# Nine token blocks of two widths (504 and 368) instead of nine of 460, a weight ring of six places instead of nine, and convolution sums written over their own input

## The chip, the cores and the metric

The kernel runs on one core of one Trainium2 chip. The metric is the device time of one execution in microseconds (us), from the first to the last instruction and what lies around them; lower is better. Several executions are timed and the median counts; one more is recorded by the profiler.

## The reference

One layer of a streaming encoder and a final RMSNorm, in float32, for a prompt of 4096 frames and a running stream of 32 more ("sample"), 4128 tokens in all:

```python
D_MODEL = 1024; D_A = D_B = 512; D_IN = 4 * D_A + 3 * D_B        # 3584
hn = rms_norm(x, norm_g)
proj = jnp.einsum('btd,de->bte', hn, w_in)
h_a, b_a, c_a, z_a, a_b, g_b, z_b = jnp.split(proj, SPLITS, axis=-1)
conv_a, new_a = causal_dwconv(hist_a, c_a * h_a, conv_a_w)       # 3 taps
out_a = b_a * conv_a * jax.nn.silu(z_a)
v_b = a_b * jax.nn.sigmoid(g_b)
conv_b, new_b = causal_dwconv(hist_b, v_b, conv_b_w)             # 31 taps
s_b = jax.nn.silu(layer_norm(conv_b + conv_b_bias, ln_b_g, ln_b_b))
out_b = s_b * jax.nn.silu(z_b)
mixed = jnp.concatenate([out_a, out_b], axis=-1)
y = rms_norm(x + jnp.einsum('bte,ed->btd', mixed, w_out), final_norm_g)
```

The outputs are y for both streams and the last 2 and 30 input rows of the two convolutions.

## The kernel before, in words

**Products.** Each float32 product is made of three matmuls on rounded halves (high by high, high by low, low by high), in `split_product` (L1933, L1934, L1935), so every operand of TensorE (PE) has a high part, made by ScalarE (ACT), and a low part, made by VectorE (DVE) or GpSimd (POOL) as a difference. A matmul here is 128 stationary columns against one block of tokens: its moving operand is as wide as the block.

**Blocks, units and periods.** The 4128 tokens and 12 columns of padding make nine blocks of TB = 460. The input projection runs in five units of 14 periods (`ORDER`, `ORDER4`); a period makes one pair of 128-channel tiles of the projection (`ga` the gated input of the 31-tap convolution, `hc` that of the 3-tap one, `bz` and `zz` the gates).
- Unit 0 (periods 0 to 13) is blocks 0 and 1, computed plainly: four tiles of 24 matmuls a period, 1344 in all; the first two tiles are 448 wide, since the padding is left out. Beside it the weights of each period are loaded, split and added up into the seven forms that Strassen's scheme needs, and stored to DRAM (`weight_forms`).
- Units 1 to 3 (periods 14 to 55) are two blocks each by one level of Strassen's scheme: seven products (P1 to P7) of 12 matmuls instead of eight, 84 matmuls a period, 3528 in all. The weight form of each product comes back from DRAM into `w_ring`, a ring of nine places, in the order of the products; a load waits for the product that held its place.
- Unit 4 (periods 56 to 69, "late") is the last block, computed plainly: 48 matmuls a period, 672 in all, as 56 half tiles. Their weights are loaded raw (`load_late`), then split by ACT and POOL (`late_low`).
- The output stage multiplies `mixed` by `w_out` in row tiles of 128 tokens, 48 matmuls of 512 columns each, with the LayerNorm steps of a token block `L` of 512 in between. Its first row tiles need the LayerNorm of block 0 (`first_ln`), which DVE does in periods 63 to 69, and whose last step `b_low` (L1765) releases the second group of matmuls.

**DVE.** For each of the 20 jobs (a unit by a group of 128 channels) DVE makes 31 taps, each one instruction as wide as the unit (L1701 the first, L1704 the others), that add into PSUM; the last tap writes `conv_b_out`, which is stored to DRAM. DVE works strictly in program order: how many taps stand in each period is a number of `tap_quota` (10 in most periods of units 0 to 3, 12 in unit 4, 7 in period 55), and a job's taps can't begin before its input `v` is made. Beside the taps stand the low parts of the weights (L1534), the 3-tap convolution (L1647, L1650), the products of tiles (L1612 to L1668), and at the ends of the units the sums and low parts of the next unit's x (L1543 to L1562).

**SyncE (SP)** issues all DMAs in one order, and waits in it.

Of the kernel before, what the change touches and what calls it, by code (L numbers as in the profile page):

```python
# [10 lines left out]
P = 128  # L11
# [10 lines left out]
BLOCKS = 9  # L22
TB = 460
PAD = BLOCKS * TB - SEQ - SAMPLE
S0, P0 = PAD, PAD + SAMPLE
TOK = BLOCKS * TB
STAT_COLS = 4
STAT_ROWS = TB // STAT_COLS
# [114 lines left out]
ACC_W = [SAMPLE + HB + 2 * TB - P0, 2 * TB, 2 * TB, 2 * TB, TB]  # L143
CA_W = [SAMPLE + HA + 2 * TB - P0, 2 * TB, 2 * TB, 2 * TB, TB]
VW, UW = 968, 928
VP, UP = HB + SAMPLE + HB, HA + SAMPLE + HA
BLK0 = TB - P0


def tap_quota(n):  # L150
    u, g = divmod(n, G14)
    if n == 0:
        return 0
    if n == III - 1:
        return 7
    if g == G14 - 1 and u < 3:
        return 1
    if g == 0 and u < 4:
        return 3
    return 10 if u < 4 else 12  # L160
# [33 lines left out]
ACC_BANK, STAT_BANK = 6, 7  # L194
FIRST_BANK = [7, 6]
# [3 lines left out]
def build_program(nc, A):  # L199
    ctx = ExitStack()  # L200
    with ctx:
# [9 lines left out]
        def sem(name):  # L211
# [5 lines left out]
        rstd_d = nc.dram_tensor("rstd_spill", [1, BLOCKS * P * STAT_COLS], F32).ap()  # L217
# [30 lines left out]
        acc = sb("conv_b_out", [P, 944], F32, early)  # L248
        sets = sb("sets", [P, 2, 4, TB], F32, early)
        ca = sb("conv_a_acc", [P, 2 * TB], F32, early)  # L250
        u = sb("u", [P, UW], F32, early)
        row = sb("x_row", [P, D], F32, early)
        spread = sb("rstd_spread", [P, TB + 4], F32, early)
        xf, xf_f32 = sb_two("xf", [P, 7, 2 * HALF, TB], early)
        st = sb("x_raw", [P, 4, HALF, TB], F32, early)
        ring, ring_f32 = sb_two("w_ring", [P, 9, 2, HC], early)
        early.close()

        sb("late_gap_a", [P, 2 * VW + 944])
# [13 lines left out]
        MIX = [mix1, mix2]  # L273
        MIX_F32 = [mix1_f32, mix2_f32]
# [1924 lines left out]
```

## Time and profile before

| | |
|---|---|
| three timed runs | 1564.76, 1566.05, 1567.96 us; median 1566.05 |
| profiled execution | 1561.36 us, of which span 1559.6 us |
| PE busy | 99% of the span |
| granted clock, mean | 0.999 of full speed |
| unit 0 begins, ends | 23.8, 301.5 us |
| units 1 to 3 end | 1041.5 us |
| unit 4 and the first output matmuls end | 1190.4 us |

The profiled execution is 4.7 us below the median. The span is cut by the starts of PE's first matmuls of a unit. PE's records of one matmul overlap, so its own cost is read as the distance between the starts of two, or as a stretch of time divided by the matmuls in it.

### The profile page before, as it was taken

To read this page: it belongs to the slowest core of one execution; us is meant where nothing else is said; L and a number is where in the kernel's file an instruction comes from. 1 tells how busy PE (TensorE), PEld (TensorE's weight loads), DVE (VectorE), ACT (ScalarE), POOL (GpSimd) and SP (SyncE) were. 2 spreads that over 40 slices of the span, in tenths; PEclk is the share of its full clock that TensorE was granted. 3 is DMA by queue.
4 is the path that set the end of the run, shared out by engine and by line. 5 is a ranking of instruction groups with operands and counts; after the bars stand their busy time and mean duration, and the time that the engine had idled before them with its cause. 6 is when DMAs were issued, how large, how long until landed. Compare 5 with 4: busy or idle time off the path is not lost. (4 is left out here: it accounts for less than half of the span.)

```text
span 1559.6 us, 19243 instructions
## 1 busy us (share of the span) xinstructions
PE 1537.6 (99%) x7244; PEld 1358.4 (87%) x7244; DVE 1262.9 (81%) x1175; ACT 537.6 (34%) x780; POOL 578.4 (37%) x494
## 2 busy tenths in 40 slices
PE   6999999999999999999999999999999999999998
PEld 6999999988888888888888888888898888888886
DVE  7699799998878998869798888789896677787853
ACT  5443433332242333332253312234533323323221
POOL 2766969112313121132221141146964233332320
PEclk9999999999999999999999999999999999999999
DMA  4987978788987789897779877757645433445441
GB/s 164 337 320 279 339 266 317 261 276 287 292 276 241 232 250 301 288 289 247 233 231 298 255 239 246 215 174 221 203 121 192 162 126 138 168 162 188 142 142 69
DMA packets 109648, 358.03 MB, mean 230 GB/s; under 512 B 16676, under 2 KB 20644, under 8 KB 105976
## 3 DMA queue, kind: packets, MB, share of 16 engines
q1 hardware_dynamic: 109560, 356.86, 68.8%
q8 instruction: 55, 0.90, 0.2%
q14 instruction: 33, 0.27, 0.0%
HBM read 263.02 MB, written 93.79 MB: 229 GB/s over the span
## 5 line engine op out<-in xcount | busy, mean ns | idle before, releaser
L1704 DVE SCALAR_TENSOR_TENSOR ps<-v,conv_b_taps,ps 128x920 f32<-128x920 f32 (+2 forms) x580 | 630.9, 1088 | 17.8
L1933 PE MATMUL ps<-xf,w_ring 128*128 128x460 f32 (+1 forms) x1624 | 602.8, 371 | 1.0 <-issue 0.8
L1935 PE MATMUL ps<-xf,w_ring 128*128 128x460 f32 (+1 forms) x1624 | 602.6, 371 | 0.0
L1934 PE MATMUL ps<-xf,w_ring 128*128 128x460 f32 (+1 forms) x1624 | 600.8, 370 | 0.0
L1933 PEld LDWEIGHTS ps<-xf,w_ring 128*128 128x128 f32 x1624 | 305.4, 188 | 35.2 <-issue 2.1
L1934 PEld LDWEIGHTS ps<-xf,w_ring 128*128 128x128 f32 x1624 | 305.4, 188 | 34.0
L1935 PEld LDWEIGHTS ps<-xf,w_ring 128*128 128x128 f32 x1624 | 304.9, 188 | 34.2
L1268 ACT ACTIVATE sets<-ps 128x460 f32<-128x460 f32 x168 | 92.9, 553 | 488.7 <-PE ps L1935 488.5
L1074 POOL TENSOR_TENSOR sets<-sets 128x460 f32<-128x460 f32 x42 | 56.2, 1337 | 414.9 <-ACT sets L1268 414.9
L1933 PE MATMUL ps<-w_out_split,mixed 128*128 128x512 f32 x528 | 206.0, 390 | 0.0
L1934 PE MATMUL ps<-w_out_split,mixed 128*128 128x512 f32 x528 | 205.7, 390 | 0.0
L1935 PE MATMUL ps<-w_out_split,mixed 128*128 128x512 f32 x528 | 205.5, 389 | 0.0
L1933 PEld LDWEIGHTS ps<-w_out_split,mixed 128*128 128x128 f32 x528 | 99.1, 188 | 21.2 <-DVE mixed L1765 0.5
L1935 PEld LDWEIGHTS ps<-w_out_split,mixed 128*128 128x128 f32 x528 | 99.1, 188 | 20.8
L1934 PEld LDWEIGHTS ps<-w_out_split,mixed 128*128 128x128 f32 x528 | 99.1, 188 | 20.5
L1477 ACT ACTIVATE ps<-h_rows 128x1024 f32<-128x1024 f32 x32 | 33.0, 1030 | 200.0 <-DVE h_rows L1851 200.0
L945 POOL TENSOR_TENSOR row_mean_sq_eps<-row_mean_sq,rms_eps 128x1 f32<-128x1 f32 x32 | 8.4, 264 | 228.4 <-ACT ps L1477 228.3
L1014 POOL TENSOR_TENSOR w_ring<-w_ring_f,w_ring 128x512 fp32r<-128x512 f32 x56 | 74.8, 1355 | 43.6 <-ACT w_ring L1228 43.6
L1933 PE MATMUL ps<-xf 128*128 128x448 f32 (+1 forms) x224 | 82.7, 369 | 0.0
L1935 PE MATMUL ps<-xf 128*128 128x448 f32 (+1 forms) x224 | 82.6, 369 | 0.0
L1934 PE MATMUL ps<-xf 128*128 128x448 f32 (+1 forms) x224 | 82.2, 367 | 0.0
L971 POOL TENSOR_TENSOR x_raw<-x_raw,rstd_spread 128x460 f32<-128x460 f32 x56 | 66.5, 1220 | 40.2 <-DMA rstd_spread<-rstd_spill 40.2
(166 smaller groups left out, 1650.2 us busy)
## 6 DMA issues: line engine op xcount, KB each, us to landing
w_ring<-weight_forms SPq DMA_DIRECT2D x294, 512.0 KB, 5.3
x_rows_again<-in_x_prompt SPq DMA_DIRECT2D x32, 512.0 KB, 4.3
out_y_prompt<-h_rows SPq DMA_DIRECT2D x32, 512.0 KB, 3.0
weight_forms<-xf SPq DMA_DIRECT2D x7, 2048.0 KB, 13.3
weight_forms<-w_ring SPq DMA_DIRECT2D x7, 2048.0 KB, 14.7
w_ring_f<-in_w_in SPq DMA_DIRECT2D x56, 256.0 KB, 3.1
xf_f<-in_w_in SPq DMA_DIRECT2D x26, 512.0 KB, 9.0
x_row<-in_x_prompt SPq DMA_DIRECT2D x28, 460.0 KB
```

The source lines that it names most:

```text
L945: pool.tensor_tensor(mean_sq[0:rows, r:r + 1], ssq[0:rows, r:r + 1], add, ALU.add).then_inc(h_ms, 1)
L971: pool.tensor_tensor(part, part, spread[:, 0:TB], ALU.mult).then_inc(x_scaled, 1)
L1014: pool.tensor_tensor(ring[:, slot, 1, :], ring_f32[:, slot, 1, :], ring[:, slot, 0, :].bitcast(F32), ALU.subtract).then_inc(late_lo, 1)
L1074: pool.tensor_tensor(sets[:, s, QC, :], sets[:, s, QC, :], sets[:, s, QD, :], ALU.add).then_inc(c22_made, 1)
L1268: act.activation(sets[:, n % 2, quarter, :], ps[:, bank, 0:TB], ACT.Copy).then_inc(copied, 1)
L1477: act.activation(out_pair(2)[0:rows, :], hrow[0:rows, s, :], ACT.Square, scale=RMS_SCALE, accum_out=ssq[0:rows, s:s + 1]).then_inc(h_sumsq, 1)
L1704: dve.scalar_tensor_tensor(dst, window, wb[:, j, k:k + 1], part, ALU.mult, ALU.add).then_inc(taps_done, 1)
L1933: pe.matmul(out, ahi, bhi, start=(start and x == 0), stop=False, skip_group_check=goes_on)
L1934: pe.matmul(out, ahi, blo, start=False, stop=False, skip_group_check=goes_on)
L1935: mm = pe.matmul(out, alo, bhi, start=False, stop=(stop and x == len(terms) - 1), skip_group_check=goes_on)
```

## The change

- **Widths.** Blocks 0, 1 and 8 (units 0 and 4) are 368 tokens, blocks 2 to 7 (the Strassen units) 504. There is no padding. The number of matmuls is the same. The taps are 766, 1008 and 368 columns wide instead of 938, 920 and 460.
- **Taps.** `tap_quota` gives 9 instead of 10 in the middle periods of unit 0. The last tap writes into `v`, over its own input, and `conv_b_out` is gone; `v` then waits for that store, two jobs earlier.
- **Ring.** `w_ring` has six places. The weight forms of unit 0 that had lain in it lie in `xf` now, the raw weights in four halves of the ring.
- **Unit 4.** Of its 56 half tiles, 21 load their weights from the stored forms (`late_form`), already split; 35 are still split anew.
- **Places.** The buffers of the output stage are laid out anew, the halves of `mixed` apart.

```diff
-BLOCKS = 9
-TB = 460
-PAD = BLOCKS * TB - SEQ - SAMPLE
+BLOCKS, TB, PAD = 1, SEQ + SAMPLE, 0
+NARROW, WIDE = 368, 504
+WIDTH = [NARROW] * 2 + [WIDE] * 6 + [NARROW]
+UNIT_WIDTH = [NARROW, WIDE, WIDE, WIDE, NARROW]
-ACC_W = [SAMPLE + HB + 2 * TB - P0, 2 * TB, 2 * TB, 2 * TB, TB]
+ACC_W = [HB + 2 * NARROW, 2 * WIDE, 2 * WIDE, 2 * WIDE, NARROW]
 def tap_quota(n):
-    return 10 if u < 4 else 12
+    return 9 if u == 0 else 10 if u < 4 else 12
+SLOTS = 6
-        acc = sb("conv_b_out", [P, 944], F32, early)
-        ring, ring_f32 = sb_two("w_ring", [P, 9, 2, HC], early)
+        ring, ring_f32 = sb_two("w_ring", [P, SLOTS, 2, HC], early)
+        def late_form(r):
+            return r % 4 == 0 or (r % 4 == 3 and r >= 2 * G14)
         def wait_v_free(eng, job):
-                eng.wait_ge(taps_done, KB * (job - 1))
+                eng.wait_ge(conv_out, conv_sent(job - 2))
             def load_w(g):
-                    done = 1 if g == 2 else g
-                    sp.wait_ge(w_sum, 4 * done)
-                    sp.wait_ge(w_lo_w, 2 * done)
+                    sp.wait_ge(w_sum, 4 * (g - 1))
+                    sp.wait_ge(w_lo_w, 2 * (g - 1))
-                if q >= 9:
-                    sp.wait_ge(product_done, q - 8)
+                if q >= SLOTS:
+                    sp.wait_ge(product_done, q - SLOTS + 1)
             def load_late(r):
+                if late_form(r):
+                    load_ring(g, r % 4, late_slot(r))
+                    return
             def tap(job, k):
-                dst = acc[:, 0:w] if k == KB - 1 else part
+                dst = v[:, job % 2, 0:w] if k == KB - 1 else part
             def standing_part(n, t, rs):
-                    mm = split_product(ps[:, bank_of(n, t), cols], terms, r == 0, r == 3)
+                    mm = split_product(ps[:, bank_of(n, t), 0:NARROW], terms, r == 0, r == 3)
             def late_tile(n, t):
-                    pe.wait_ge(late_lo, r + 1)
+                    if late_form(r):
+                        pe.wait_ge(ring_in[late_slot(r)], late_weights_in(r))
+                    else:
+                        pe.wait_ge(late_lo, LATE_AT[r])
```

**DVE at the boundary of unit 3 and unit 4.** Rows of its order before, from the low parts of the last block's x to the first taps of unit 4 (`ps` is the sum in PSUM, a name with a width each):

```order
L1569 TENSOR_TENSOR xf<-x_raw,xf 128x1840 x2
L1704 SCALAR_TENSOR_TENSOR ps<-v,conv_b_taps,ps 128x920 x7
L1577 TENSOR_TENSOR sets<-ps,sets 128x460
L1580 TENSOR_TENSOR sets<-ps,sets 128x460
L1668 TENSOR_TENSOR conv_a_acc<-ps,conv_a_acc 128x460
L1687 TENSOR_TENSOR sets<-conv_a_acc,sets 128x920
L1704 SCALAR_TENSOR_TENSOR ps<-v,conv_b_taps,ps 128x920 x4
L1704 SCALAR_TENSOR_TENSOR conv_b_out<-v,conv_b_taps,ps 128x920
L1621 TENSOR_TENSOR v<-ps,sets 128x460
L1701 TENSOR_SCALAR ps<-v,conv_b_taps,conv_b_bias_sb 128x460
L1704 SCALAR_TENSOR_TENSOR ps<-v,conv_b_taps,ps 128x460 x11
```

The same place of the changed kernel:

```order
L1605 TENSOR_TENSOR xf<-x_raw,xf 128x1472 x2
L1741 SCALAR_TENSOR_TENSOR ps<-v,conv_b_taps,ps 128x1008 x7
L1613 TENSOR_TENSOR sets<-ps,sets 128x504
L1616 TENSOR_TENSOR sets<-ps,sets 128x504
L1704 TENSOR_TENSOR conv_a_acc<-ps,conv_a_acc 128x504
L1723 TENSOR_TENSOR sets<-conv_a_acc,sets 128x1008
L1741 SCALAR_TENSOR_TENSOR ps<-v,conv_b_taps,ps 128x1008 x9
L1741 SCALAR_TENSOR_TENSOR v<-v,conv_b_taps,ps 128x1008
L1657 TENSOR_TENSOR v<-ps,sets 128x368
L1738 TENSOR_SCALAR ps<-v,conv_b_taps,conv_b_bias_sb 128x368
L1741 SCALAR_TENSOR_TENSOR ps<-v,conv_b_taps,ps 128x368 x11
```

Ahead of unit 4's first `v` DVE has ten wide taps where it had five, since unit 0 has 108 taps instead of 113 and the later periods the same number as before; and each is wider.

**SP at the same place.** Its last loads of unit 3 and the first of unit 4 before:

```order
L692 DMA w_ring<-weight_forms 128x1024
L714 DMA w_ring_f<-in_w_in 128x512 x9
L767 DMA w_out_split_f<-in_w_out 128x1024
L714 DMA w_ring_f<-in_w_in 128x512 x3
L728 DMA outa_spill<-sets 128x920
```

And in the changed kernel:

```order
L736 DMA w_ring<-weight_forms 128x1024 x5
L759 DMA w_ring_f<-in_w_in 128x512 x3
L736 DMA w_ring<-weight_forms 128x1024
L759 DMA w_ring_f<-in_w_in 128x512
L810 DMA w_out_split_f<-in_w_out 128x1024
L759 DMA w_ring_f<-in_w_in 128x512 x2
L736 DMA w_ring<-weight_forms 128x1024
L771 DMA outa_spill<-sets 128x1008
```

Every fourth of unit 4's loads is a form of 512 KB instead of 256 KB raw, and the loads run six places ahead of PE instead of nine.

## Rows read from the trace of the kernel before

**Rows 1.** The page, parts 1 and 2: busy time by engine, granted clock by slice.

```profile
PE 1537.6 (99%) x7244; PEld 1358.4 (87%) x7244; DVE 1262.9 (81%) x1175; ACT 537.6 (34%) x780; POOL 578.4 (37%) x494
...
PEclk9999999999999999999999999999999999999999
```

**Rows 2.** Windows by stage: length, then busy us of PE, PEld, DVE, ACT, POOL.

```profile
0.00:23.80 23.80, 9.45 (x44) 9.40 (x45) 13.37 (x15) 14.38 (x13) 4.12 (x13) 1.00 0.70 253
23.80:301.50 277.70, 277.70 (x1355) 253.49 (x1355) 247.61 (x216) 110.66 (x137) 192.88 (x128) 1.00 0.78 286
301.50:1041.50 740.00, 739.00 (x3529) 662.93 (x3528) 622.88 (x578) 238.53 (x388) 165.13 (x177) 1.00 0.81 259
1041.50:1190.40 148.90, 148.89 (x717) 133.18 (x715) 134.18 (x168) 64.21 (x95) 108.78 (x80) 1.00 0.58 174
1190.40:1559.60 369.20, 362.57 (x1604) 299.37 (x1604) 244.84 (x201) 109.86 (x148) 107.48 (x97) 1.00 0.43 150
```

**Rows 3.** Windows inside unit 0, unit 1 and the output stage; last columns clock, DMA share, GB/s.

```profile
64.40:281.70 217.30, 217.30 (x1057) 198.30 (x1056) 200.78 (x168) 86.05 (x109) 163.89 (x110) 1.00 0.82 297
320.10:530.10 210.00, 210.00 (x1005) 188.64 (x1004) 174.62 (x169) 64.78 (x110) 50.02 (x57) 1.00 0.84 271
1300.00:1490.00 190.00, 190.00 (x838) 156.97 (x837) 143.27 (x111) 61.54 (x79) 64.39 (x53) 1.00 0.44 156
```

**Rows 4.** Timeline of PE in unit 4: start, duration, line, tiles, width.

```profile
1142.37 0.95 PE L2061 MATMUL ps<-ones,ln_tmp_b_f 128*128 128x1 f32 x8
1143.18 0.46 PE L1933 MATMUL ps<-xf,w_ring 128*128 128x460 f32 x1
```

**Rows 5.** Timeline of PE in the first period of unit 1.

```profile
313.80 0.37 PE L1935 MATMUL ps<-xf,w_ring 128*128 128x460 f32 x1
314.99 0.45 PE L1933 MATMUL ps<-xf,w_ring 128*128 128x460 f32 x1 [0.82 <-issue]
```

**Rows 6.** Timeline of DVE at the boundary of unit 0 and unit 1.

```profile
292.39 2.07 DVE L1543 TENSOR_TENSOR xf_f<-x_raw 128x1840 f32<-128x1840 f32 x1
...
310.84 2.07 DVE L1555 TENSOR_TENSOR x_raw<-x_raw 128x1840 f32<-128x1840 f32 x1
312.83 4.12 DVE L1562 TENSOR_TENSOR xf<-x_raw,xf 128x1840 fp32r<-128x1840 f32 x2
```

**Rows 7.** Timeline of DVE in unit 4, idle before and its releaser in brackets.

```profile
1045.51 2.09 DVE L1687 TENSOR_TENSOR sets<-conv_a_acc,sets 128x920 f32<-128x920 f32 x1 [1.88 <-POOL conv_a_acc L1056]
1047.53 4.82 DVE L1704 SCALAR_TENSOR_TENSOR ps<-v,conv_b_taps,ps 128x920 f32<-128x920 f32 x4
...
1055.06 8.08 DVE L1704 SCALAR_TENSOR_TENSOR ps<-v,conv_b_taps,ps 128x460 f32<-128x460 f32 x11
...
1064.51 2.34 DVE L1650 SCALAR_TENSOR_TENSOR conv_a_acc<-u,conv_a_taps,conv_a_acc 128x460 f32<-128x460 f32 x2
...
1083.22 0.76 DVE L1701 TENSOR_SCALAR ps<-v,conv_b_taps,conv_b_bias_sb 128x460 f32<-128x460 f32 x1 [0.62 <-POOL v L1030]
...
1097.62 0.46 DVE L1647 TENSOR_SCALAR conv_a_acc<-u,conv_a_taps 128x460 f32<-128x460 f32 x1 [4.97 <-POOL u L1038]
...
1188.08 2.29 DVE L1765 TENSOR_TENSOR mixed<-conv_b,mixed 128x2048 fp32r<-128x2048 f32 x1 [1.99 <-ACT mixed L1337]
```

**Rows 8.** Groups of DVE by form in the window of unit 4: count, busy us, mean ns.

```profile
L1704 DVE SCALAR_TENSOR_TENSOR ps<-v,conv_b_taps,ps 128x460 f32<-128x460 f32 x116 | 81.4, 701 | 3.8
L1650 DVE SCALAR_TENSOR_TENSOR conv_a_acc<-u,conv_a_taps,conv_a_acc 128x460 f32<-128x460 f32 x8 | 12.4, 1544 | 0.3
```

**Rows 9.** DMA from 64 to 184 us, in unit 0: all packets, then the queue's MB and share.

```profile
DMA packets 7808, 37.38 MB, mean 311 GB/s; under 512 B 1554, under 2 KB 1682, under 8 KB 6264
...
q1 hardware_dynamic: 7800, 37.28, 85.4%
```

**Rows 10.** The page, part 6: form loads, count, KB each, median us from issue to landing.

```profile
w_ring<-weight_forms SPq DMA_DIRECT2D x294, 512.0 KB, 5.3
```

More of the change, by code:

```diff
@@ L313, in standing_x, with last_x, quarter, first_raw @@
         def standing_x(b, part, a, e):
-            return xf[:, 3 + 2 * b + part, a:e, :]
+            return x_flat((X0_AT, X1_AT)[b] + XW * part)[:, a:e, :]
+        def last_x(part, a, e):
+            return x_flat(XW * part)[:, a:e, :]
+        def quarter(n, q, blocks=1):
+            w = UNIT_WIDTH[0] if unit(n) == 0 else WIDE
+            return sets[:, n % 2, w * q:w * q + (w * (blocks - 1) + UNIT_WIDTH[unit(n)])]
+        def first_raw(b, h, a=0, e=HALF):
+            return st[:, 2 * b + h, a:e, 0:NARROW]
         def bank_of(n, t):
@@ L322, in set_banks @@
             return [3 * (n % 2) + b for b in range(3)]
-        def tile_cols(n, t):
-            return slice(PAD if unit(n) == 0 and t < 2 else 0, TB)
         def product(n, i):
@@ L360, in late_split @@
             if g < 0:
-                return range(4) if part == 2 else ()
-            if g == G14 - 1:
-                return ()
-            return (range(4 * g + 4, 4 * g + 6), [4 * g + 6], [4 * g + 7])[part]
+                some = range(4) if part == 2 else ()
+            elif g == G14 - 1:
+                some = ()
+            else:
+                some = (range(4 * g + 4, 4 * g + 6), [4 * g + 6], [4 * g + 7])[part]
+            return [r for r in some if not late_form(r)]
         const_in = sem("const_in")
@@ L400, in build_program @@
         late_lo = sem("w_late_lo")
-        ring_in = [sem(f"w_ring_in_{s}") for s in range(9)]
+        ring_in = [sem(f"w_ring_in_{s}") for s in range(SLOTS)]
         tile_done = sem("tile_done")
@@ L1040, in second_block @@
             def second_block(n):
-                uu, q, s = unit(n), which(n), n % 2
+                uu, q = unit(n), which(n)
                 if uu in (0, 4) or kind(n) == "zz":
                     return
-                second = sets[:, s, QC, :]
+                second = quarter(n, QC)
                 pool.wait_ge(c22_made, n - II + 1)
@@ L1653, in gate_b @@
             def gate_b(n):
-                uu, j = unit(n), which(n)
+                uu, j, w = unit(n), which(n), UNIT_WIDTH[unit(n)]
                 after(period_of("hc", uu, j), "t2")
```

351 lines of the change are left out of this document (181 added, 170 removed).

## The prediction

> **What bounds the kernel now.** I read the page first: PE is busy 99% of the span, and the granted clock is at its full level, 2.4 GHz, in all 40 slices [rows 1]. So the time is the number of matmuls by what each costs PE, plus the few stalls, and the clock is no term of the change. The windows by stage then say where there is anything else [rows 2]: up to 23.8 us PE waits for the first x; unit 0 takes 277.7 us without a gap; units 1 to 3 take 740.0 us, 1.0 of them idle; unit 4 takes 148.9 us, and the output stage 369.2 us with 6.6 us idle. What one matmul costs is read from windows inside the stages, length divided by count [rows 3]. In unit 0 it is 217.3/1056 = 205.8 ns for 454 columns on the average (448 and 460 by turns). A column at 2.4 GHz is 0.417 ns, so 189.2 ns are columns and 16.6 ns are fixed. In unit 1 it is 210.0/1004 = 209.2 ns; less 191.7 for 460 columns, 17.5 fixed. In the output stage it is 190/837 = 227.0 ns; less 213.3 for 512 columns, 13.7 fixed. (A few records are missing or of other shapes; 1 count in 1000 is 0.2 ns.)
>
> Could the load of the stationary operand become the limit when the columns fall to 368? Eight matmuls of one column, each with a new operand, take 0.81 us from start to next start [rows 4], 0.10 us each. A matmul of 368 columns needs 153 ns for its columns alone, so that limit is not reached.
>
> The second engine is DVE: busy 92% of the steady window of unit 0, 83% in unit 1's [rows 3], 90% in unit 4 [rows 2]. It works in order, so wherever PE gets quicker, DVE is what to look at.
>
> **The change, part by part.** The columns: 672 x 448 + 672 x 460 + 3528 x 460 + 672 x 460 = 2,542,176 before, and 1344 x 368 + 3528 x 504 + 672 x 368 = 2,520,000 now. That is 22,176 fewer, 9.2 us. All else is the fixed part, which is paid as often as before, and the stages in which PE may not be the bound.
>
> *Start.* The first x is narrower by a fifth: loads, squares and scaling of two blocks. PE's first product comes at 23.8 us; most of that is latency and DVE's and ACT's 13 to 14 us of work [rows 2], of which x is perhaps half. I take -1.3 us (bounds -2.5 and 0).
>
> *Unit 0.* 1344 matmuls of 368 columns: 153.3 ns and a fixed part that no row shows at this width. Its bounds are 13.7 and 17.5 ns [rows 3], and I take the middle, 15.2: 168.5 ns, 226.5 us, 0.3 more for the joins, against 277.7. That is -50.9 us (bounds -53 and -47.8), if nothing else holds the period of 96 x 168.5 = 16.2 us; that is a rival below.
>
> *Boundary of unit 0 and unit 1.* DVE makes the forms of the next x there, one after another [rows 6]: 2.07 us each of 1840 elements. They become 2016 elements, 2.26 us, while the period of unit 0 in which they stand shrinks from 19.8 to 16.2 us. PE's stall at the fourth product is 314.99 - 313.80 less a matmul, 1.0 us, marked as issue [rows 5]; DVE's last two low parts start at 312.83. DVE is later by six operations of 0.19 us, 1.1 us, and a little of the lost 3.6 us of the period. I take +1.5 us (bounds 0 and +8, the latter if nearly all of the lost period and the longer forms come back as stall: 3.6 + twelve operations by 0.19, and a first form load of the ring that is as late again).
>
> *Units 1 to 3.* 3528 matmuls of 504 columns: 210.0 ns, and the fixed part of the same stage, 17.5 ns: 227.5 against 209.2 (209.3 with the joins). 3528 x 18.2 ns = +64.2 us. The lower bound is the fixed part of the output stage, 13.7: +50.9; above, I allow half of these 3.8 ns between stages once more, 19.4 ns: +70.9. Here the ring of six places costs nothing: it holds 6 x 12 x 227.5 ns = 16.4 us of products where nine held 22.6, and a form lands 5.3 us after its issue [rows 10]. If a load is behind others by less than 11 us, nothing waits. DVE gains room: by the tap costs below, a tap goes from 1.205 to 1.295 us, 7%, and a period of 84 matmuls from 17.6 to 19.1, 9%.
>
> *Unit 4.* PE alone would need 672 x (153.3 + 17.5) ns = 114.8 us, and as before 5.4 for 24 matmuls of the output that stand in the window and 2.6 for LayerNorm's, 122.8 against 148.9: -26.1. But here DVE must be through its order before the first LayerNorm's low part lets the second output group begin. It is just in balance now: the low part starts at 1188.08 after a wait for ACT [rows 7] and ends at 1190.4, where the window ends. So I sum DVE's chain from 1041.5 to 1190.4:
> - In place of five taps of 920 there are ten of 1008. A tap is 4.82/4 = 1.205 us at 920 and 8.08/11 = 0.735 at 460 [rows 7], which is 1.02 ns a column; so 1.295 at 1008 and 0.641 at 368. Five more: +6.5. Five wider, with the products ahead of them: +0.7.
> - 120 taps of 460 columns (116 of one group and the 4 last ones [rows 8]) become 368: 120 x 0.094 = -11.3. Some 34 other operations of that width: -3.2.
> - DVE waits for POOL's edges of u and v, 4.97 and 0.62 us [rows 7]. Being later by 7 us it finds them made: -5.6.
> - The eight accumulations of the 3-tap convolution took 12.4 us [rows 8] where 2.34 a pair would be 9.4 [rows 7], beside POOL's work, which falls as 21 of 56 subtractions go: -2.1.
>
> The sum is -15.0: the stage takes 133.9 us, 11 more than PE would. The bounds are -12 and -17, and -26 if DVE were not the bound. On those eight accumulations: the Trainium skill (SBUF — State Buffer, section "SBUF: two separate sides") says that VectorE and GpSimd exclude each other from a shared port pair for whole instructions. By that rule the whole 3.0 us of excess would be given back if POOL were silent, and none if it is not; the sum would be 0.9 lower or 2.1 higher.
>
> The loads of unit 4 run six places ahead: 6 half tiles of 12 x 171 ns are 12.3 us. A raw piece must be loaded, and be split by ACT and POOL in that time; a form of 512 KB lands after 5.3 us [rows 10]. POOL is busy 108.8 of 148.9 us now [rows 2]; with 35 of 56 low parts it would be about 80 of 134. I count nothing.
>
> *Output.* The operands' places change, the number and width of matmuls don't. The fixed part differs by 1 to 4 ns between stages [rows 3], and only the high halves of one buffer, 512 of 1584 matmuls, come to a place unlike before: 512 x 3.5 ns = +1.8 us (bounds 0 and +3).
>
> *In-place last tap.* `v` of a job waits for the store of the job two before, which ends two periods or more ahead. Below nothing it can't be: no instruction goes. I count 0.
>
> **Sum.** -1.3 - 50.9 + 1.5 + 64.2 - 15.0 + 1.8 = +0.3 us. On the profiled execution, 1561.36 us (span 1559.6), that is 1561.7; the median of the runs stands 4.7 higher, so **1566.4 us** is forecast. About 0.2%, 3.1 us, is what a measurement can tell from no change. Some 9 us saved in columns are lost again in unit 4, where DVE holds PE.
>
> **Rivals.**
>
> *A smaller fixed part (faster).* If it is as small at 504 and 368 columns as at 512, 13.7 ns, units 1 to 3 take 3528 x 3.8 = 13.4 us less and unit 0 1344 x 1.5 = 2.0 less: 1551 us. For it: 504 is near 512. Against it: the stage, with its operands, stays, and the stage had 17.5. The Trainium skill (TensorE: Matmul & The Clock Gate, section "Back-to-back issue gap") gives an isolated gap of N/2.4 + 2.5 ns. By that rule the fixed part would be smaller still in every stage; the trace's 227.0 ns at 512 columns, where the rule has 215.8, speaks against it.
>
> *Unit 4 is not held by DVE (faster).* If taps and waits shrink more than I sum, or the low part need not wait for the whole order, -26 instead of -15: 1555.5 us. Against it: DVE is busy 134.2 of 148.9 us and the low part stands behind all taps.
>
> *Unit 0 is held by something other than PE (slower).* This is one mechanism: the weights' loading, splitting and storing doesn't shrink with the tokens. From 64 to 184 us 37.3 MB moved with the DMA engines 85.4% busy [rows 9]; six periods now last 97 us, the bytes are about 36.3 MB (if an eighth is x and results, a fifth narrower), and at the rate of full business (311/0.854 = 364 GB/s) they need 99.7 us. DVE: 200.8 us in 11 periods [rows 3] are 18.3 each; one tap less (1.2), nine narrower by 172 columns (1.6) and some 0.6 on other operations leave 14.9 of 16.2 us. It decides if a period takes over 16.2 us; at 17.1 in eleven periods it is +10: 1576.5 us. For it: those shares. Against it: a share of 85% need not be a rate's limit, and the raw weights still have two places each, so a late one has cover.
>
> *A larger fixed part at 504 (slower).* 19.4 ns in place of 17.5: +6.7 us, 1573 us. For it: the fixed part isn't the same from stage to stage, so it hangs on something besides the count, the operands' places perhaps, and these change. Against it: 512 columns have the smallest of all.
>
> **Chances and range.** The forecast, 0.38 (its own range 1562 to 1572; within 0.2% in 0.27, faster 0.04, slower 0.07); smaller fixed part 0.16; unit 4 free of DVE 0.12; unit 0 held 0.20; larger fixed part 0.14, of which 0.02 is within 0.2%. Faster by over 0.2%: 0.04 + 0.16 + 0.12 = 0.32. Within: 0.29. Slower: 0.07 + 0.20 + 0.12 = 0.39. The range 1553 to 1578 leaves out most of the first rival and the ends of the two slower ones, together 0.2.
>
> **What would show it.** In the changed trace: starts of PE's matmuls 168.5 ns apart in unit 0 and 227.5 in units 1 to 3; unit 0 some 227 us long without gaps, with a stall of 2 to 3 us in all at its end; in unit 4 DVE without idle time, PE with about 11 us of it, most just before the second output group; the output stage as long as before within 3 us. It is wrong if PE idles for DVE, POOL or a load in unit 0, if the fixed parts differ by over 2 ns, or if unit 4's PE has no gap.

## The result

The changed kernel takes 1587.08 us (median of 4 runs, 1579.86 to 1590.26) against 1566.76 us (1564.76 to 1567.96) of the kernel before on the same chip: the ratio is 1.0125, with a 95% interval of 1.0088 to 1.0161. It is 20 us slower where 1566.4 us, no change, was forecast, and outside the range of 1553 to 1578. Its profiled execution is the quickest of the four, 1579.86 us with a span of 1577.9; the other three have a mean granted clock of 0.990 to 0.993 where this one has 0.994 and the kernel before 0.999.

The changed kernel's windows by stage, cut at the same places as before: length, then busy us of PE, PEld, DVE, ACT and POOL, clock, DMA share, GB/s.

```profile
0.00:21.85 21.85, 8.82 (x45) 8.76 (x45) 11.76 (x16) 12.83 (x13) 4.24 (x13) 1.00 0.72 241
21.85:267.75 245.90, 230.33 (x1355) 229.16 (x1354) 214.24 (x210) 108.10 (x138) 193.12 (x128) 0.98 0.85 316
267.75:1073.67 805.92, 805.71 (x3528) 663.49 (x3529) 667.93 (x579) 247.80 (x384) 175.00 (x178) 1.00 0.77 242
1073.67:1206.38 132.71, 124.33 (x717) 120.30 (x715) 119.02 (x172) 54.61 (x77) 80.38 (x58) 0.99 0.77 234
1206.38:1577.90 371.52, 364.98 (x1604) 299.34 (x1604) 245.01 (x201) 109.74 (x148) 107.72 (x97) 1.00 0.43 150
```

Beside [rows 2] that is, stage by stage, in us (from the starts to a hundredth, so that a row can differ by 0.1 from the windows):

| stage | forecast | measured |
|---|---|---|
| start | -1.3 | -2.0 |
| unit 0 and its end | -49.4 | -31.7 |
| units 1 to 3 | +64.2 | +65.9 |
| unit 4 | -15.0 | -16.2 |
| output | +1.8 | +2.4 |
| sum | +0.3 | +18.3 |

All but one row of the table are within 2 us. Nearly the whole miss, 17.7 of 18.0 us, is in unit 0, in which PE now idles 15.6 us and runs for a while at a lower clock. What PE waited for, in all of the span (us in total, times, longest):

```profile
PE ps L1970 <- DVE v L1650: 7.6, 2, 4.7
PE ps L1970 <- POOL w_ring L1052: 6.7, 6, 3.0
PE ps L1970 <- DMA w_ring<-weight_forms: 4.9, 2, 4.0
PE ps L1970 <- DVE conv_a_acc L1698: 3.9, 1, 3.9
```

The first and the last line are three stalls in unit 0, each at the fourth tile of a period (4, 7 and 11): the starts of two matmuls in succession are 3.2, 4.3 and 5.0 us apart there. L1650 and L1698 are DVE's products that empty a PSUM bank which that tile is to fill. The 4.0 us of the third line are PE's wait for the first weight form of unit 1: SP stores the last forms of unit 0 at 254.46 us, right behind POOL's last low parts, waits for them to land, and loads the first one back at 263.14. POOL's line is unit 4. PE's timeline at the third stall:

```profile
224.90 0.67 PE L1970 MATMUL ps<-xf 128*128 128x368 f32 x1 [4.72 <-DVE v L1650]
225.37 0.51 PE L1971 MATMUL ps<-xf 128*128 128x368 f32 x1
225.68 0.51 PE L1972 MATMUL ps<-xf 128*128 128x368 f32 x1
225.99 0.51 PE L1970 MATMUL ps<-xf 128*128 128x368 f32 x1
```

and the windows around it:

```profile
224.90:230.70 5.80, 5.80 (x19) 5.80 (x20) 5.76 (x5) 1.06 (x1) 5.64 (x4) 0.51 0.97 378
230.70:240.00 9.30, 9.30 (x58) 9.30 (x57) 9.05 (x12) 3.80 (x5) 9.22 (x7) 1.00 0.69 283
```

After the stall matmuls start 0.31 us apart, at a granted clock of 0.51, which is the level of 1.2 GHz; from 230.7 us on it is 1.00 again, and 9.30/58 = 0.16 us. So 19 matmuls cost some 2.6 us more. This stall is paid once as idle time and once more as clock. The one at 154.3 us is too (0.63 over the 4.5 us behind it, 17 matmuls, some 1.7 us more); the shortest, with 2.9 us of idle time, is not: the 3.9 us behind it have a clock of 1.00. Together the clock costs some 4.3 us, and 226.0 us (unit 0 without a stall, e5 below) and 15.6 and 4.3 make the 245.9. The prediction, "the clock is no term of the change", had this wrong as soon as there are long stalls.

Why is DVE late? Its timeline ahead of the second stall, from the low parts of one pair of weights to the product that PE waits for:

```profile
120.81 1.28 DVE L1713 TENSOR_TENSOR sets<-conv_a_acc,sets 128x32 f32<-128x32 f32 x1
...
122.81 9.46 DVE L1741 SCALAR_TENSOR_TENSOR ps<-v,conv_b_taps,ps 128x766 f32<-128x766 f32 x9
...
135.51 3.46 DVE L1570 TENSOR_TENSOR xf<-w_ring_f,xf 128x1024 fp32r<-128x1024 f32 x2 [2.29 <-ACT xf L1259]
138.90 1.62 DVE L1683 TENSOR_SCALAR conv_a_acc<-u,conv_a_taps 128x738 f32<-128x738 f32 x1
140.56 3.85 DVE L1686 SCALAR_TENSOR_TENSOR conv_a_acc<-u,conv_a_taps,conv_a_acc 128x738 f32<-128x738 f32 x2
144.33 9.45 DVE L1741 SCALAR_TENSOR_TENSOR ps<-v,conv_b_taps,ps 128x766 f32<-128x766 f32 x9
...
153.79 0.50 DVE L1698 TENSOR_TENSOR conv_a_acc<-ps,conv_a_acc 128x336 f32<-128x336 f32 x1
...
254.69 0.60 DVE L1683 TENSOR_SCALAR conv_a_acc<-u,conv_a_taps 128x738 f32<-128x738 f32 x1 [1.74 <-issue]
```

Nearly no idle time, and two things to see. First, from the end of one period's nine taps (132.2) to the end of the next one's (153.7) are 21.5 us, in a period that PE could do in 16.2. Second, some operations are much longer than their size says: 1.28 us for 32 columns, where a product of 336, with one operand in PSUM, takes 0.50; 1.62 us for the first tap of the 3-tap convolution, and 0.60 us for the same instruction at 254.69 us, where POOL has just run out of work. POOL during the 3-tap convolution:

```profile
137.97 2.15 POOL L1035 TENSOR_TENSOR xf_f<-xf_f,w_ring_f 128x512 f32<-128x512 f32 x1
140.08 1.60 POOL L1036 TENSOR_TENSOR xf_f<-w_ring_f 128x512 f32<-128x512 f32 x1
141.76 1.86 POOL L1038 TENSOR_TENSOR xf_f<-w_ring_f,xf_f 128x512 f32<-128x512 f32 x1
143.70 5.34 POOL L1044 TENSOR_TENSOR xf<-xf_f,xf 128x1024 fp32r<-128x1024 f32 x2
```

These are its sums of weights and their low parts, the same number and width as before the change. Three causes could stand behind the stalls: DVE has too many instructions for a 16 us period; its instructions, and POOL's, are lengthened by each other; or the weights come too late from DRAM (the DMA share is 0.85, and the row of 135.51 shows a wait for them). The experiments take them one by one.

These causes are coupled, because SP waits in its one order. What SP waited for in POOL, in unit 0:

```profile
SPq L732 <- POOL xf L1044: 83.8, 12, 9.2
...
SPq L692 <- POOL x_rstd_columns L993: 15.6, 2, 10.0
SPq L723 <- POOL xf_f L1038: 11.0, 1, 11.0
```

That is 110.4 us, and the next raw weights stand behind it. Ahead of the second stall SP stands until 128.83 us for POOL's `x_rstd_columns` and issues the raw weights only at 129.29; POOL then has its longest wait for weights:

```profile
127.77 1.03 POOL L993 TENSOR_TENSOR x_rstd_columns<-x_mean_square_eps,minus_half 126x4 f32<-126x4 f32 x1
...
135.76 2.13 POOL L1033 TENSOR_TENSOR xf_f<-w_ring_f 128x512 f32<-128x512 f32 x1 [6.78 <-DMA w_ring_f<-in_w_in]
```

So a busy POOL can delay itself, ACT and DVE through SP as well. No experiment below changes SP's order in unit 0.

### The profile page after: what moved, and what is told of

The parts are those of the page before. It is cut to its first block and busy times, and to the rows that moved or that the text cites. A ratio compares the mean times of both kernels' runs of the same rounds, so it can differ in the third digit from the quotient of the medians.

```text
span 1577.9 us, 19186 instructions
## 1 busy us (share of the span) xinstructions
PE 1534.2 (97%) x7244; PEld 1321.1 (84%) x7244; DVE 1258.0 (80%) x1175; ACT 533.1 (34%) x759; POOL 560.5 (36%) x473
## 5 line engine op out<-in xcount | busy, mean ns | idle before, releaser
L1741 DVE SCALAR_TENSOR_TENSOR ps<-v,conv_b_taps,ps 128x1008 f32<-128x1008 f32 (+2 forms) x580 | 630.9, 1088 | 17.5
L1970 PE MATMUL ps<-xf,w_ring 128*128 128x504 f32 (+1 forms) x1400 | 536.3, 383 | 12.0 <-POOL w_ring L1052 6.7
L1971 PE MATMUL ps<-xf,w_ring 128*128 128x504 f32 (+1 forms) x1400 | 533.6, 381 | 0.0
L1972 PE MATMUL ps<-xf,w_ring 128*128 128x504 f32 (+1 forms) x1400 | 532.0, 380 | 0.0
L1970 PEld LDWEIGHTS ps<-xf,w_ring 128*128 128x128 f32 x1400 | 263.8, 188 | 62.9 <-issue 8.3
L1972 PEld LDWEIGHTS ps<-xf,w_ring 128*128 128x128 f32 x1400 | 263.7, 188 | 48.6
L1971 PEld LDWEIGHTS ps<-xf,w_ring 128*128 128x128 f32 x1400 | 263.8, 188 | 45.4
L1304 ACT ACTIVATE sets<-ps 128x504 f32<-128x504 f32 x168 | 99.1, 590 | 545.3 <-PE ps L1972 545.1
L1970 PE MATMUL ps<-w_out_split,mixed_hi 128*128 128x512 f32 x528 | 206.7, 392 | 0.6 <-DVE mixed_lo L1802 0.6
L1972 PE MATMUL ps<-w_out_split,mixed_lo 128*128 128x512 f32 x528 | 206.5, 391 | 0.0
L1971 PE MATMUL ps<-w_out_split,mixed_hi 128*128 128x512 f32 x528 | 206.2, 390 | 0.0
L1970 PE MATMUL ps<-xf 128*128 128x368 f32 x448 | 150.4, 336 | 11.6 <-DVE v L1650 7.6
L1972 PE MATMUL ps<-xf 128*128 128x368 f32 x448 | 149.4, 333 | 0.0
L1971 PE MATMUL ps<-xf 128*128 128x368 f32 x448 | 148.4, 331 | 0.0
L1970 PEld LDWEIGHTS ps<-w_out_split,mixed_hi 128*128 128x128 f32 x528 | 99.1, 188 | 22.6 <-DVE mixed_lo L1802 1.0
L1972 PEld LDWEIGHTS ps<-w_out_split,mixed_lo 128*128 128x128 f32 x528 | 99.1, 188 | 21.6
L1971 PEld LDWEIGHTS ps<-w_out_split,mixed_hi 128*128 128x128 f32 x528 | 99.1, 188 | 21.6
L1970 PEld LDWEIGHTS ps<-xf 128*128 128x128 f32 x448 | 85.7, 191 | 12.5 <-DVE v L1650 8.2
```

What stands on the lines that cost most here:

```text
L1304: act.activation(quarter(n, q), ps[:, bank, 0:WIDE], ACT.Copy).then_inc(copied, 1)
L1741: dve.scalar_tensor_tensor(dst, window, wb[:, j, k:k + 1], part, ALU.mult, ALU.add).then_inc(taps_done, 1)
L1970: pe.matmul(out, ahi, bhi, start=(start and x == 0), stop=False, skip_group_check=goes_on)
L1971: pe.matmul(out, ahi, blo, start=False, stop=False, skip_group_check=goes_on)
L1972: mm = pe.matmul(out, alo, bhi, start=False, stop=(stop and x == len(terms) - 1), skip_group_check=goes_on)
```

## The experiments

Below, "unit 0" is the time from its first matmul to unit 1's, "unit 4" from its first matmul to the second output group, all from the profiled execution. Four executions with an unaltered unit 0 (the changed kernel, e2, e7, e11) have 245.9, 250.5, 244.0 and 243.7 us there: a difference below 7 us says nothing. Five with an unaltered unit 4 (the changed kernel, e1, e4, e5, e12) have 132.7, 132.0, 131.9, 132.6 and 135.4 us.

### e1: the taps moved out of the heavy periods

```diff
+    if 0 < n < G14 - 1:
+        return (0, 11, 12, 5, 11, 11, 5, 7, 9, 12, 5, 9, 10)[n]
```

> The changed kernel with the same 108 taps in unit 0, placed otherwise: 5 instead of 9 in the periods in which DVE also has the 3-tap convolution (3, 6, 10), 9 to 12 in the others. Theory A (DVE's order is fuller than PE's period just there, and a tile is not emptied in time): the three gaps of 3.1, 4.1 and 4.9 us at the fourth tile of periods 4, 7 and 11 go, and with them the stretches at half clock behind them; unit 0 takes 228 to 234 us instead of 245.9, the kernel 1565 to 1572 us profiled. Rival B (the transfers of weights can't keep a 16 us period, whatever DVE does): unit 0 stays at 240 or more and the gaps turn up elsewhere. Unit 4 as before: 132 to 133 us from its first matmul to the second output group.

Ratio to the kernel before 1.0120 (1.0097 to 1.0144), profiled span 1576.1; unit 0 244.3 us. The stalls moved instead of going: starts are 3.3, 2.7 and 1.7 us apart in periods 3, 6 and 10, and 7.8 at unit 1's first product. Theory A in the form "only those periods are too full" falls: the work that is too long is spread over the unit.

### e2 and e3: more taps in units 1 to 3, or in unit 0

```diff
-    return 9 if u == 0 else 10 if u < 4 else 12
+    return 9 if u == 0 else 11 if u < 4 else 12      # e2
+    return 10 if u < 4 else 12                       # e3
```

> The changed kernel with 11 instead of 10 taps a period in units 1 to 3, so that 2 instead of 10 wide taps are left for unit 4. Theory A (in unit 4 the backlog of wide taps delays the store of the last Strassen job, on which SP stands before it issues the next weights, and a ring of six places doesn't cover that): the four gaps of 0.8 to 1.4 us in period 59 go, and perhaps the one of 3.2 us in period 62; unit 4 takes 120 to 126 us instead of 132.7, the kernel about 8 to 10 us less than the changed one. Rival B (the ring's loads are late by themselves, DMA or POOL): the gaps stay and the kernel gains under 3 us. Rival C (DVE has no room for 11 taps in units 1 to 3): these units get longer than 805.9 us.

Ratio 1.0128 (1.0097 to 1.0160). The gaps of period 59 are gone, that of period 62 (3.2 us) is not; unit 4 takes 129.8 us instead of 132.7. Units 1 to 3 take 811.3 us instead of 805.9, with starts 1.2 and 1.8 us apart at the fifth and sixth product of each later unit, for which DVE makes the operands: rival C is right as well. What is won in unit 4 is lost there.

> The changed kernel with the quota of unit 0 put back to 10: 113 taps in unit 0, and 5 instead of 10 wide ones in unit 4. Theory A (DVE's order bounds unit 0): five more taps of 1.05 us, about +4 to +6 us in unit 0 (250 to 252 us) with more half-clock stretches; unit 4 gains 3 to 6 us. The two about cancel: 1576 to 1582 us profiled. Rival B (transfers bound unit 0): unit 0 stays at 246, and the kernel gains the 3 to 6 us of unit 4.

Ratio 1.0126 (1.0100 to 1.0153). Unit 0 takes 252.2 us, now with stalls in periods 4, 5, 7, 11 and 12, and unit 4 128.0 us with no gap in period 59. Theory A's numbers for both, and the two cancel as expected; but 252.2 is only 1.7 us above e2's 250.5, whose unit 0 is unaltered. In unit 0 the five stalls speak for theory A, the length alone doesn't. Five wide taps in unit 4, as in the kernel before, are few enough.

### e4: a quarter of the raw weights

```diff
-                    sp.dma_start(raw_weights(g, f), src).then_inc(w_in[f][g % 2], 16)
+                    cut = slice(0, HC if g < 2 else HC // 4)
+                    sp.dma_start(raw_weights(g, f)[:, :, cut], src[:, :, cut]).then_inc(w_in[f][g % 2], 16)
```

> The changed kernel loads only a quarter of the raw weights in unit 0 from the third pair on (three quarters of them are left as they lie in the buffer, so the results are not the reference's); 0.75 MB of about 4.6 MB a period less, and each load is there sooner. Theory A (DVE's own order is too long by 3 to 5 us in the heavy periods, of which at most 2.3 us are waits for the high parts of weights): the gaps shrink by up to 2.3 us each but at least two of the three stay; unit 0 takes 236 to 243 us. Rival B (late weights are the cause): all gaps go, unit 0 takes 225 to 230 us.

One run: 1570.9 us, unit 0 238.2 us. The stall of period 7 is gone, that of period 4 is 4.3, that of period 11 is 2.2 us, that at unit 1's first product 4.1. Theory A's numbers: 7.7 of the 19.9 us to a unit without stalls, a little over the spread. So late weights seem to have a part in it, and the smaller one.

### e5: POOL's work on the weights at a quarter of its width

```diff
-                low = lambda c: chunks(g, c, c + 1, True)[:, 0, 1, :]
-                w11, w12, w21, w22 = [raw_chunk(g, c) for c in range(4)]
+                cut = slice(0, HC if g < 2 else HC // 4)
+                low = lambda c: chunks(g, c, c + 1, True)[:, 0, 1, cut]
+                w11, w12, w21, w22 = [raw_chunk(g, c)[:, cut] for c in range(4)]
```

and the same `cut` in `sums_low` and in ACT's high parts of the sums.

> The changed kernel with POOL's sums of weights and their low parts a quarter as wide in unit 0 from the third pair on (and ACT's high parts of them; three quarters are left as they lie, so the results are not the reference's). DMA and DVE have the same instructions as before. Theory C (DVE has the instructions it had, but beside a busy POOL they take longer: 1024-wide low parts 1.83 us on the average, 3-tap accumulations 1.67, a 32-wide product 1.27): the low parts fall to 1.2 to 1.45 us, the accumulations to about 1.0, the 32-wide product to 0.2, and unit 0's three gaps go: 226 to 231 us. Rival A (DVE's own work is too long for a 16 us period whatever POOL does): durations fall by less than a tenth, unit 0 stays above 240 us.

One run: 1557.4 us. Unit 0's window:

```profile
21.11:247.09 225.98, 225.98 (x1355) 225.97 (x1354) 195.11 (x212) 94.10 (x139) 112.68 (x128) 1.00 0.91 348
```

The groups of DVE by form in it (count, busy us, mean ns, idle before):

```profile
L1745 DVE SCALAR_TENSOR_TENSOR ps<-v,conv_b_taps,ps 128x766 f32<-128x766 f32 x101 | 103.0, 1020 | 3.3
L1574 DVE TENSOR_TENSOR xf<-w_ring_f,xf 128x1024 fp32r<-128x1024 f32 x27 | 37.2, 1399 | 15.4 <-ACT xf L1263 15.1
L1690 DVE SCALAR_TENSOR_TENSOR conv_a_acc<-u,conv_a_taps,conv_a_acc 128x738 f32<-128x738 f32 x8 | 8.4, 1048 | 0.3
```

The same groups of the changed kernel in its unit 0:

```profile
L1741 DVE SCALAR_TENSOR_TENSOR ps<-v,conv_b_taps,ps 128x766 f32<-128x766 f32 x101 | 103.0, 1020 | 3.3
L1570 DVE TENSOR_TENSOR xf<-w_ring_f,xf 128x1024 fp32r<-128x1024 f32 x27 | 48.8, 1835 | 12.2 <-ACT xf L1259 12.1
L1686 DVE SCALAR_TENSOR_TENSOR conv_a_acc<-u,conv_a_taps,conv_a_acc 128x738 f32<-128x738 f32 x8 | 13.4, 1674 | 0.3
```

Unit 0 has no gap, and takes 226.0 us where 226.5 was forecast for a PE that nothing holds. DVE has the same instructions with the same widths. The taps, which read one operand from PSUM, take the same 1020 ns; the low parts and the accumulations, with both operands in SBUF, fall from 1835 to 1399 and from 1674 to 1048 ns. The DMA share is 0.91 at 348 GB/s, and though POOL waits 68.9 us for raw weights now, PE never does, so the transfers were not the bound. Theory C: POOL's work on the weights is what unit 0 waits for. By which way is not parted: its own length, what it does to DVE, and what it does to SP, whose waits for POOL fall from 110.4 to 50.3 us. The edit also takes 14 us from ACT, whose high parts of the sums shrink with it (108.1 to 94.1 us); ACT is busy less than half of the time in either, but stands in the chain between POOL and DVE, and its share was not tried by itself. The 32-wide products didn't all fall as expected: 0.45, 0.72 and 1.26 us, where they were 1.26 to 1.28. The rule of the Trainium skill that the prediction named for unit 4 (SBUF — State Buffer, section "SBUF: two separate sides") says which operations of VectorE suffer beside GpSimd: those with two SBUF inputs, and those in a mode that takes two ports. The low parts and accumulations agree with the first; that rule was needed in unit 0, where it wasn't applied.

### e6: six places in the kernel before

```diff
-                if q >= 9:
-                    sp.wait_ge(product_done, q - 8)
+                if q >= 6:
+                    sp.wait_ge(product_done, q - 5)
-                    q = 7 * (n - II) + i + 9
+                    q = 7 * (n - II) + i + 6
```

and likewise in `load_late`.

> The kernel before, with its loads of the ring in units 1 to 4 issued six places ahead of PE instead of nine, and nothing else changed. Theory A (six places are enough at the old widths, where a half tile takes 2.5 us and DVE has five wide taps left at unit 4's start; the gaps need the change's shorter half tiles and its backlog): units 1 to 3 as long as before, unit 4 within 1.5 us, the kernel +0 to +3 us. Rival B (the six places are the whole cause of unit 4's gaps): gaps of 1 to 3 us in periods 59 and 62, and one at unit 1's start; +5 to +9 us.

Ratio 1.0001 (0.9989 to 1.0014), by ten runs. Units 1 to 3 take 740.0 us, unit 4 149.5. The shorter ring costs nothing at the old widths: theory A.

### e7: SP's order in unit 4

```diff
-                if g < KC:
-                    load_wo(g)
-                    if c == 1:
+                    if c == 3:
                         store_convs(n)
+                        if g < KC:
+                            load_wo(g)
```

> The changed kernel with SP's order in unit 4 altered: in each period the stores of finished convolutions and the load of w_out come behind the four loads of weights instead of ahead of them and between them. Theory A (the weights are late because SP stands in front of them, for DVE's last tap in period 59 and for ACT's split of w_out in 62): the gaps of period 59 (four, 3.9 us in all) and 62 (3.2) shrink by at least 4 us together; unit 4 takes 124 to 129 us instead of 132.7. Rival B (transfers or POOL are late by themselves): the gaps stay within 1 us, 132 us.

One run: unit 4 takes 134.2 us; starts 2.2 us apart in period 59 and 2.1 in 62, and a new 3.0 in period 69. The gaps of the two periods shrink by some 3 us together, less than the 4 expected, and the unit isn't shorter. The expectation failed. A likely reason, read from the order: the wait isn't saved by standing behind four loads, since the next period's loads stand behind it. The store that SP waits for is late because of DVE; e2 and e3 remove it by the taps.

### e8: fewer taps in unit 0

```diff
+    if 0 < n < G14 - 1:
+        return (0, 8, 9, 6, 9, 9, 6, 9, 9, 9, 6, 9, 8)[n]
-    return 9 if u == 0 else 10 if u < 4 else 12
+    return 12 if u == 4 else 11 if g < 10 else 10
```

with SP's order of e7.

> The changed kernel with 97 instead of 108 taps in unit 0, fewest (6) in the periods with the 3-tap convolution; 11 a period instead of 10 in the first ten periods of units 1 to 3, and 10 in the last three, so that 4 wide taps are left for unit 4; and SP's order in unit 4 as in the run before this one. If DVE's total is the bound in unit 0 and SP's order in unit 4: eleven taps less are 11.6 us of DVE; unit 0 takes 230 to 236 us, unit 4 120 to 126, and the kernel is 1558 to 1566 us, within half a per cent of the kernel before. If something else binds unit 0 (POOL or transfers), it stays at 240 or more and the kernel at 1570 or more.

Ratio 1.0111 (1.0093 to 1.0129), unit 0 246.7 us, unit 4 129.7. Eleven taps less in unit 0 (ten in the group of full ones, 91 instead of 101, which is 10.3 us of DVE), and the unit isn't shorter. Its stalls inside are smaller (three, with starts 2.4 us apart, in periods 7 and 11), but at unit 1's first product starts are 10.6 us apart, where PE waits 10.3 us for DVE's last low parts of x (L1600). SP stores the last forms, behind POOL's last low parts, at 254.36 us, where it was 254.46 in the changed kernel: POOL's work ends when it did, whatever DVE was spared. What DVE waited for in it:

```profile
DVE xf L1572 <- ACT xf L1261: 19.4, 8, 5.0
...
DVE conv_a_acc L1685 <- POOL u L1075: 3.1, 1, 3.1
```

The time won became waiting for the high parts of weights, which in turn (50.6 us of ACT's waits) stand behind POOL's sums. So DVE's number of instructions alone is not the bound either.

### e9: the quarter of POOL's work, in the kernel before

The edit of e5.

> The kernel before with POOL's sums of weights and their low parts (and ACT's high parts of them) a quarter as wide in unit 0 from the third pair on, as in the run e5 (three quarters are left as they lie; the results are not the reference's). If PE is the bound of unit 0 before, as its 277.6 us without a gap say: unit 0 stays at 277 to 278 us and the kernel within 1 us, though DVE's low parts and 3-tap accumulations shorten from 1.84 and 1.99 us to about 1.4 and 1.2. If POOL already costs something there, unit 0 gets shorter by over 1 us.

One run: 1562.5 us beside 1563.6 of the kernel before, unit 0 278.4 us, no gap. DVE's accumulations fall from 1990 to 1252 ns, so POOL lengthened them there too; but in that kernel PE bounds unit 0, and POOL and DVE fit a period of 19.8 us.

### e10: both causes away

The edit of e5, and units 1 to 3 with the quotas of e8.

> The changed kernel with both causes taken away: POOL's sums and low parts of weights a quarter as wide in unit 0 (e5; results not the reference's), and 11 instead of 10 taps a period in the first ten periods of units 1 to 3, which leaves 2 to 4 wide taps for unit 4. If these two are what took the gain: unit 0 226 us, units 1 to 3 804 to 806, unit 4 to the second output group 124 to 128 (only the gap in period 62 and the ends are left), the kernel 1549 to 1555 us, 0.5 to 0.9% faster than the kernel before: about the 9 us of columns. If there is a third cause, it is not faster than 1557.

1555.4 us, ratio 0.9941 (0.9922 to 0.9960): this one is faster. Unit 0 227.5 us, units 1 to 3 804.3, unit 4 129.1, which is 1 us more than expected; the median is 0.4 us above the expected range. The gaps that are left are in period 62 (starts 3.3 us apart) and in 69 (2.2). It leaves work out, so it is no kernel to use; it shows that the columns' gain is there, and that these two edits together give it back.

### e11: no stored forms in unit 4

```diff
-            return r % 4 == 0 or (r % 4 == 3 and r >= 2 * G14)
+            return False
```

> The changed kernel with all 56 half tiles of unit 4 split anew, as before, in place of 35. Theory A (unit 4's gaps come from a raw piece having to be loaded and split within six places, and each stored form spares a split): more gaps, POOL with 21 more subtractions of 1.3 us; unit 4 takes 135 to 142 us to the second output group instead of 132.7. Rival B (the forms' 512 KB transfers are what comes late): the gaps shrink, unit 4 takes 125 to 130.

One run: 1589.1 us, unit 4 145.6 us, more than expected. What PE waited for from 1073 to 1210 us:

```profile
PE ps L1970 <- POOL w_ring L1052: 12.4, 5, 5.0
PE ps L1970 <- POOL mixed_lo L1135: 3.0, 1, 3.0
```

The stored forms save 13 us there. Six places by themselves don't make the splitting late: in e6 all 56 half tiles are split within six places of 2.5 us. What the change adds in unit 4 is shorter half tiles (2.0 us) and loads that start late; which of them counts was not parted.

### e12: DVE's low parts of weights at a quarter of their width

```diff
-                    dve.tensor_tensor(chunks(g, 2 * f, 2 * f + 2)[:, :, 1, :], raw_weights(g, f),
+                    cut = slice(0, HC if g < 2 else HC // 4)
+                    dve.tensor_tensor(chunks(g, 2 * f, 2 * f + 2)[:, :, 1, cut], raw_weights(g, f)[:, :, cut],
```

> The changed kernel with DVE's low parts of the weights a quarter as wide in unit 0 from the third pair on (three quarters left as they lie; the results are not the reference's); POOL, ACT and DMA as in the changed kernel. DVE has some 33 us less. Theory C1 (DVE and POOL hold each other up, so relief of either helps): POOL's operations shorten too, from 1.7 and 2.55 us, by a tenth or more; unit 0 takes 226 to 234 us. Rival C2 (POOL's own chain of sums and low parts is too long for 16 us, whatever DVE does): POOL's durations stay and unit 0 takes over 238.

One run: 1572.0 us, unit 0 235.4 us, between the two theories. The low parts take 27.8 us instead of 48.8. POOL's first sum falls from a mean of 1746 to 1412 ns, its low parts from 2555 to 2468 ns; its whole busy time in the unit from 193.1 to 174.2 us with the same instructions. The influence goes both ways. Half the loss comes back with DVE's relief, all of it with the edit of POOL's and ACT's work.

## Why the prediction was wrong, point by point

*Cost of a matmul: right.* For 504 columns 227.5 ns were forecast; a window inside unit 1 of the changed kernel has

```profile
300.00:500.00 200.00, 200.00 (x880) 164.87 (x879) 160.34 (x146) 58.11 (x95) 50.62 (x52) 1.00 0.81 253
```

200/879 = 227.5 ns. For 368 columns 168.5 was forecast; e5's unit 0 without a gap gives 225.98/1344 = 168.1, with the joins and the eleven other matmuls of the window in it. From 30.06 to 40.06 us of the changed kernel 60 products start in 10.00 us, 166.7 ns each, which leaves 13.4 for the fixed part. So both rivals on the fixed part fall at 504 columns; at 368 it is near the smaller one, which the prediction prices at 2 us in unit 0; for unit 4 it took 17.5, which is, by an estimate from these 13.4, 2.8 us too much. Units 1 to 3 came out at +65.9 for +64.2; in e5, without the slow stretch at their start, they take 804.3 us, which is +64.3.

*Unit 0: the step that failed.* The term of -50.9 us, "if nothing else holds the period", left out what does hold it: the work on the weights. With the boundary the stage gave -31.7 instead of -49.4. The rival that named it ("the weights' loading, splitting and storing doesn't shrink with the tokens", chance 0.20) gave +10 us; it was 18 with the boundary and the clock's share. Two steps in its working were wrong. It put DVE at 14.9 of 16.2 us by taking a tap away in each period, while the diff's order shows 108 instead of 113 taps in all, five and not eleven: the group of full taps went from 127.1 to 103.0 us. And it summed DVE alone from durations of [rows 3] as if these were its own, and left POOL out. 1835 ns of a low part, or 1674 of an accumulation, hold POOL's share, and POOL's hold DVE's. The same eleven periods (2 to 12) as in [rows 3], of the changed kernel and of e5:

```profile
55.06:247.58 192.52, 180.96 (x1057) 180.06 (x1057) 176.03 (x168) 82.95 (x108) 161.78 (x108) 0.97 0.92 342
```

```profile
54.52:231.09 176.57, 176.57 (x1057) 176.56 (x1057) 159.04 (x171) 69.92 (x110) 88.48 (x113) 1.00 1.00 381
```

DVE is busy 16.0 us a period there, not 14.9, in a period that should take 16.2 and takes 17.5; in e5 it is 14.5. POOL's 161.8 us are 14.7 a period; before the change it was 14.9 (163.9 in [rows 3]), of 19.8. Both engines wait for each other's results and for SP on top of that, and this chain doesn't fit 16.2 us. The transfers, on which the rival put its first number, were only a part (e4): in e5 they run at a share of 1.00 and 381 GB/s, and PE has no gap.

*Boundary of unit 0 and unit 1.* Forecast +1.5, bounds 0 and 8. In the changed kernel starts are 4.3 us apart at the first product, where before they were 1.2 apart at the sixth [rows 5] (the prediction calls it the fourth), and some ten matmuls run at the lower clock after it. In e5, which gets there without delays, there is no such gap. So it isn't the longer forms that cost; it follows from unit 0.

*Unit 4: the size right by luck, the mechanism not.* -15.0 was forecast and -16.2 measured, but "DVE without idle time" isn't so: DVE is busy 119.0 of 132.7 us. Of PE's 8.4 us of idle time 6.7 are waits for POOL's low parts of weights, and only 0.6 for DVE. "I count nothing" for the loads was the wrong sentence. The backlog of ten wide taps that DVE brings along does cost, by another way: SP stands before DVE's last tap of the last Strassen job, the weights behind it are issued late, and the lead of six places, 12 us, doesn't cover that. SP's rows around that wait, and ACT's wait for the weights:

```profile
1085.86 0.33 SPq L759 DMA_DIRECT2D w_ring_f<-in_w_in  x1
1092.69 0.34 SPq L799 DMA_DIRECT2D conv_spill<-v  x1
```

```profile
1099.61 0.63 ACT L1265 ACTIVATE w_ring<-w_ring_f 128x512 fp32r<-128x512 f32 x1 [8.66 <-DMA w_ring_f<-in_w_in]
```

SP issues nothing for 6.8 us. e2 and e3 take the backlog away and the gaps of period 59 with it: 129.8 and 128.0 us, where the unaltered units 4 have 131.9 to 135.4. e6 shows that the ring alone doesn't make them. In period 62 POOL does LayerNorm's sums ahead of the low parts that PE needs:

```profile
1124.01 2.43 POOL L1120 TENSOR_TENSOR ln_tmp_a_f<-conv_b 128x1024 f32<-128x1024 f32 x1
1126.52 1.29 POOL L1123 TENSOR_TENSOR ln_tmp_a_f<-ln_tmp_a_f 128x512 f32<-128x512 f32 x1
...
1130.16 2.81 POOL L1052 TENSOR_TENSOR w_ring<-w_ring_f,w_ring 128x512 fp32r<-128x512 f32 x2
```

That this order is the cause there is read from the rows and was not tried.

*Output.* +1.8 by the operands' new places for 512 matmuls, measured +2.4. It is not a third of the matmuls at 3.5 ns, but a mean of 1.7 ns over all: from 1320 to 1500 us 788 start where 794 did before, 228.4 instead of 226.7 ns each, of the same width. That the places make it was not tried. In all variants of the changed kernel but e11 this stage has 371.5 us. *In-place last tap:* no wait for the store is seen.

*What stays open.* How much of unit 0's loss is POOL's own length, how much its lengthening of DVE, how much SP's order behind POOL and how much ACT's high parts was not parted: e5 takes some of all four, e12 mostly the second. An order of SP in unit 0 that issues the raw weights ahead of its waits for POOL is the obvious run that is missing. And no whole kernel with the new widths was found that keeps up with the one before; the best, e8 (1.0111), is no better than the change itself within the intervals.

## What to carry to other kernels

When a stage is narrowed in the tokens, list what in it doesn't have that dimension (here the sums and splits of the weights), engine by engine, and put it against the new period, for every engine that feeds the bound one and not only the busiest. Where two engines lengthen each other's operations, a duration in the trace isn't one engine's cost: compare the same instruction beside an idle neighbour and beside a busy one before adding it up. A kernel that had PE at 99% had its gain in fewer columns (0.6% in e10), but PE can only take it where its suppliers had room left.

## What the runs showed of the hardware that wasn't expected

- VectorE beside a busy GpSimd: a product of 32 columns took 1.26 to 1.28 us (0.45 to 1.26 in e5, where GpSimd's work is a quarter as wide), a two-operand accumulation of 738 columns 1.67 us instead of 1.05, the single-operand instruction of 738 columns 1.62 us, and 0.60 once GpSimd had stopped. Taps with their sum in PSUM kept 1020 ns in either case.
- The granted clock was 0.51 for 5.8 us behind a stall of 4.7 us, which cost PE 2.6 us more, about half as much again; behind one of 2.9 us it stayed at 1.00. In the changed kernel's four runs the mean clock was 0.990 to 0.994, and they lie within 10.4 us; the kernel before's lie within 3.2 us in four runs, and within 5.3 to 8.9 in the 7 to 13 beside the experiments.
- TensorE's fixed part of a matmul: 13.4 ns at 368 columns (166.7 less 153.3), 17.5 at 504, and at 512 13.7 in the kernel before [rows 3] and 15.1 in the changed one (228.4 less 213.3). It didn't follow the width, and it wasn't the same in both kernels at one width.
